# RWKV mixer stages: two products move from GpSimd to VectorE, the norm's matmuls stand between the solve's scores, and parts of the next block's work stand between the recurrence's steps

## The chip, the core and the metric

The kernel runs on one core of a Trainium2 chip. Its engines are PE (TensorE), DVE (VectorE), ACT (ScalarE), POOL (GpSimd) and SP (SyncE, which here only starts DMAs). The metric is the device time of one execution in microseconds; before the change it is 3907.61 us, the median of 3 runs (3906.08 to 3911.87).

## What is computed

The program is a stack of two different two-layer blocks over 512 tokens of width 1024, with feed-forward parts of width 2816 before, between and after the mixers. Nearly all of its time is projections. The part at hand is one mixer of the second layer, RWKV-7, with 8 heads of 64:

```python
def rwkv7_mixer(p, mu, w0, wB, a0, aB, gB, k_k, k_a, r_k, ln_g, ln_b):
    p = token_shift(p, mu)
    r, k, v, wd, ad, gd = split_cols(p, RK_SIZES)
    w_raw = -jax.nn.softplus(-(w0 + jnp.tanh(wd) @ wB)) - 0.5
    decay = jnp.exp(-jnp.exp(w_raw))
    a = jax.nn.sigmoid(a0 + ad @ aB)
    kk = heads(k * k_k); kk = kk / jnp.maximum(jnp.sqrt(jnp.sum(kk * kk, -1, keepdims=True)), 1e-12)
    k = k * (1.0 + (a - 1.0) * k_a)
    def step(state, inp):
        sa = jnp.einsum('bhij,bhj->bhi', state, -kk_t)
        state = (state * w_t[:, :, None, :] + sa[..., None] * (kk_t * a_t)[:, :, None, :]
                 + v_t[..., None] * k_t[:, :, None, :])
        return state, jnp.einsum('bhij,bhj->bhi', state, r_t)
```

Beside it stands a gated linear attention (GLA), whose output o gets a norm over each head: `head_norm(o, norm_g, None, eps) * silu(og)`.

## The kernel before

The recurrence over 512 tokens is done in chunks of C = 32 tokens, four chunks to a block of P = 128, NB = 4 blocks. Inside a chunk the dependence of each token on those before it is a triangular system, which is solved for all heads and chunks at once. Four stages do this, `rwkv_features`, `rwkv_solve`, `rwkv_chunks` and `rwkv_output`; a stage is a block of the program, and none starts before all engines are through with the one before. Within a stage each engine has its own list of instructions, in the order in which the code writes them, and waits on semaphores (`wait_ge`), which others raise (`then_inc`). All data of these stages lie in one tile, `odd_arena`; `bank` are the eight banks of PSUM.

**Features.** For k in 0 to 3 (128 rows of features each) ACT computes gates, an inverse norm RN and exponentials of the summed decays (CE, CP, CI; `decays`, L1930 and on). DVE sums and multiplies: `early(k)`, then `keys(k)` (KD and BI, L1990, L1992), `factors(k)` (key times CI, BI times CI, L1997, L1999) and `bonus(k)` (L1984, from PSUM). POOL multiplies r by CE (L2019) and KD by CP (L2021). CE has two slots, so ACT's decays of k wait until r of k - 2 is scaled. PE ends with 16 matmuls that compute nothing that is used (`warm`, L400).

**Solve.** PE computes four sets of scores (L2045), two banks each, and DVE multiplies the 32x32 triangles by a mask into LT (L2113, eight instructions a set). A set writes over the banks of the last but one, so the third and fourth wait for masks. Then PE does the norm of GLA's output: for each of four heads a matmul that centres it (L2052) and one of the mean square (L2057), with ACT squaring, copying and computing the factor (L2068 to L2083, two tables of functions in turn) and POOL applying it in three products (L2098, L2100, L2103). DVE meanwhile sets T to the identity (L2116, L2118), transposes LT (L2120), and solves: 31 times a product (L2126) and a subtraction (L2129), each waiting for the last, then a transpose (L2131). PE ends with 27 filling matmuls.

**Recurrence.** For a block b of 128 tokens PE's `before(b)` computes the scores of keys against KD (`scores(b, 0)`, L2166) and transposes KD, B2 and K2 (`turn`, L2178); ACT copies each transpose out (L2268) and DVE masks the scores to M (`mask_scores`, L2329). `front(b)` transposes the values (`turn(b, 3)`), computes the two other sets of scores (A1, A2 after DVE's mask), and three products that ACT copies out (L2290). `steps(b)` runs the four chunks in order: W1 times state (L2220), DVE's SA (L2352), keys times values (L2226) and BT times SA (L2231) into bank 4, DVE's sum to the next state (L2358). POOL scales the state by the decay (L2317). `output(b)` adds into banks 5 and 2 the product of values with A2 (L2242), of SA with A1 (L2245), and of states with r (L2251); ACT copies them out (L2273). The order on PE is before(0), and for each b front(b), steps(b), before(b + 1), output(b). DVE at a block's start spreads the solved triangles into the block-diagonal BD (four copies, L2337) and masks the scores.

## Time and profile before

| | |
|---|---|
| median of 3 runs | 3907.61 us (3906.08 to 3911.87) |
| the profiled execution | 3906.92 us, its span 3905.2 us |
| busy share of the span | PE 94%, DVE 44%, ACT 35%, POOL 16% |
| mean granted TensorE clock | 0.966 of full |

The engines work side by side, so shares don't add up. A share over the whole span tells little of a stage in which the engines wait for one another; for these the profile is cut into stretches and read as a timeline. The granted clock is that of TensorE alone: 1.00 is 2.4 GHz and 0.50 is 1.2 GHz. A busy PE isn't a PE at its peak: at half clock the same matmuls are busy twice as long. The profile splits an f32 matmul into two records, so that 8 matmuls are counted x16.

### The profile page before, as it was taken

The numbers are of one execution on the slowest core, as the hardware profiler recorded it, in microseconds if no ns is written. First come the engines' busy times: TensorE is split into PE (matmuls) and PEld (weight loads), VectorE is DVE, ScalarE is ACT, GpSimd is POOL, SyncE is SP. The second block draws the span as 40 slices with busy tenths as digits, with TensorE's granted clock in tenths as the row PEclk, the third lists the DMA queues.
The fourth block names the chain that finished last, engine by engine and source line by source line (L and its number), as shares of the span: only waits on it lengthen the run. The fifth ranks groups of instructions, "written<-read, shape, count | busy, mean of one in ns | idle before, by whom it ended". The sixth has DMA issues, their size and how long they took to land. (4 is left out here: it accounts for less than half of the span.)

```text
span 3905.2 us, 46147 instructions
## 1 busy us (share of the span) xinstructions
PE 3680.2 (94%) x18324; PEld 2992.0 (77%) x18324; DVE 1712.0 (44%) x2060; ACT 1369.7 (35%) x1828; POOL 624.7 (16%) x519
## 2 busy tenths in 40 slices
PE   8999987999999999887999989998999899989998
PEld 6888865888888887465888868786888787867886
DVE  2224564322422244753422344555663435547642
ACT  2223533422332243422422243345343423454432
POOL 2112002210311030130311140003111210022110
PEclk9999998999999999887999999999999999999999
DMA  3222211222222222000222233312222323222222
GB/s 140 97 84 88 92 54 65 76 97 88 95 97 97 89 98 87 18 1 23 76 97 87 91 123 104 113 65 97 97 97 87 118 98 119 79 100 81 97 92 81
DMA packets 62088, 340.09 MB, mean 87 GB/s; under 512 B 7024, under 2 KB 11520, under 8 KB 32768
## 3 DMA queue, kind: packets, MB, share of 16 engines
q1 hardware_dynamic: 61952, 338.19, 24.6%
q8 instruction: 96, 1.57, 0.2%
q14 instruction: 40, 0.33, 0.0%
HBM read 331.87 MB, written 6.29 MB: 87 GB/s over the span
## 5 line engine op out<-in xcount | busy, mean ns | idle before, releaser
L390 PE MATMUL bank<-x_hi,w_hi 128*128 128x512 f32 (+1 forms) x3360 | 1326.5, 395 | 107.3 <-POOL x_lo L2479 48.2
L391 PE MATMUL bank<-x_lo,w_hi 128*128 128x512 f32 (+1 forms) x3360 | 1313.0, 391 | 0.0
L392 PE MATMUL bank<-x_hi,w_lo 128*128 128x512 f32 (+1 forms) x3360 | 1312.2, 391 | 0.0
L354 DVE TENSOR_TENSOR w_lo<-raw,w_hi 128x2048 fp32r<-128x2048 f32 (+2 forms) x316 | 666.7, 2110 | 911.4 <-ACT w_hi L349 896.7
L390 PEld LDWEIGHTS bank<-x_hi,w_hi 128*128 128x128 f32 x3360 | 638.7, 190 | 266.5 <-issue 99.7
L349 ACT ACTIVATE w_hi<-raw 128x2048 fp32r<-128x2048 f32 (+2 forms) x311 | 538.9, 1733 | 715.2 <-PE bank L392 709.7
L392 PEld LDWEIGHTS bank<-x_hi,w_lo 128*128 128x128 f32 x3360 | 638.4, 190 | 132.6
L391 PEld LDWEIGHTS bank<-x_lo,w_hi 128*128 128x128 f32 x3360 | 639.1, 190 | 128.9 <-issue 1.0
L390 PE MATMUL bank<-f_g_hi,w_hi 128*128 128x512 f32 (+1 forms) x770 | 288.2, 374 | 0.0
L392 PE MATMUL bank<-f_g_hi,w_lo 128*128 128x512 f32 (+1 forms) x770 | 285.6, 371 | 0.0
L391 PE MATMUL bank<-f_g_lo,w_hi 128*128 128x512 f32 (+1 forms) x770 | 285.6, 371 | 0.0
L912 DVE TENSOR_TENSOR f_prod<-f_silu,bank 128x512 f32<-128x512 f32 x88 | 60.5, 688 | 453.9 <-ACT f_silu L865 453.9
L865 ACT ACTIVATE f_silu<-bank 128x512 f32<-128x512 f32 x88 | 52.8, 599 | 579.1 <-PE bank L392 579.1
L953 POOL TENSOR_TENSOR f_g_lo<-f_prod,f_g_hi 128x512 f32 (+1 forms) x88 | 114.0, 1295 | 805.0 <-ACT f_g_hi L867 805.0
L391 PEld LDWEIGHTS bank<-f_g_lo,w_hi 128*128 128x128 f32 x770 | 145.0, 188 | 26.2 <-issue 1.0
L390 PEld LDWEIGHTS bank<-f_g_hi,w_hi 128*128 128x128 f32 x770 | 145.1, 188 | 26.0 <-issue 1.0
L392 PEld LDWEIGHTS bank<-f_g_hi,w_lo 128*128 128x128 f32 x770 | 145.0, 188 | 24.8
L390 PE MATMUL bank<-c_g_hi,w_hi 128*128 128x512 f32 x352 | 137.2, 390 | 4.8 <-DVE w_lo L354 4.8
L391 PE MATMUL bank<-c_g_lo,w_hi 128*128 128x512 f32 x352 | 137.0, 389 | 0.0
L392 PE MATMUL bank<-c_g_hi,w_lo 128*128 128x512 f32 x352 | 136.9, 389 | 0.0
L3236 ACT ACTIVATE work<-bank,cols 128x512 f32<-128x512 f32 x88 | 63.7, 775 | 180.9 <-DVE bank L3281 180.9
L3334 POOL TENSOR_TENSOR c_g_lo<-work,c_g_hi 128x512 f32 (+1 forms) x44 | 56.9, 1295 | 424.6 <-ACT c_g_hi L3245 424.6
(443 smaller groups left out, 3988.3 us busy)
## 6 DMA issues: line engine op xcount, KB each, us to landing
raw<-in_weights SPq DMA_DIRECT2D x222, 1024.0 KB, 4.8
raw<-in_weights SPq DMA_DIRECT2D x96, 704.0 KB, 4.1
raw<-in_weights SPq DMA_DIRECT2D x8, 768.0 KB, 4.2
x_kept<-X SPq DMA_DIRECT2D x2, 2048.0 KB, 10.9
X<-x_kept SPq DMA_DIRECT2D x2, 2048.0 KB, 10.0
work<-in_rpb SPq DMA_DIRECT2D x12, 256.0 KB, 5.1
stats<-in_rpb SPq DMA_DIRECT2D x12, 256.0 KB, 5.3
X<-in_x SPq DMA_DIRECT2D x8, 256.0 KB, 6.2
```

What stands on the lines that cost most here:

```text
L349: act.activation(w_hi[:, s, 0:size], raw[:, s, 0:size], ACT.Copy).then_inc(hi_ready.sem, 1)
L354: dve.tensor_tensor(w_lo[:, s, 0:size], raw[:, s, 0:size], w_hi[:, s, 0:size].bitcast(F32), ALU.subtract).then_inc(lo_ready.sem, 1)
L390: pe.matmul(out, wh[:, w], hi(k), start=first and n == 0, stop=False, skip_group_check=not group)
L391: pe.matmul(out, wh[:, w], lo(k), start=False, stop=False, skip_group_check=not group)
L392: mm = pe.matmul(out, wl[:, w], hi(k), start=False, stop=last and n == len(kts) - 1, skip_group_check=not group)
L865: act.activation(silu[:, u, :], bank[2 * u][:, :], ACT.Silu).then_inc(act_ready.sem, 1)
L912: dve.tensor_tensor(prod[:, u, :], silu[:, u, :], bank[2 * u + 1][:, :], ALU.mult).then_inc(product_ready.sem, 1)
L953: pool.tensor_tensor(g_lo[:, j, :], prod[:, u, :], g_hi[:, j, :].bitcast(F32), ALU.subtract).then_inc(rest_ready.sem, 1)
L3236: act.activation(out[:, u, :], bank[2 * u + n][:, :], ACT.Identity, bias=ccol("conv_b_2", l * 2 * FT + off + j), scale=ccol("conv_w_2", (l ...
L3334: pool.tensor_tensor(g_lo[:, j, :], prod[:, u, :], g_hi[:, j, :].bitcast(F32), ALU.subtract).then_inc(rest_ready.sem, 1)
```

## The change

Four edits in three stages. (1) Features: POOL's two products per k are issued by DVE, inside `factors`; POOL has no work there. (2) Solve, PE: after each set of scores b comes the centring matmul of head b, and the mean square of head b - 1; the last mean square follows. (3) Solve, DVE: the two memsets of T stand before the masks. (4) Recurrence: the output's first eight matmuls (`values`) stand behind the first step, the next block's first scores behind the second and third in halves, the first transpose behind the fourth; DVE spreads one of the next block's four triangles after each step's state, and after the fourth masks the next scores. These scores use banks 1 and 7 in place of 0 and 1, so the second transpose, which writes bank 7, waits for the mask.

```diff
                     def factors(k):
-                        key, ci = RK[:, 4 + k, :], CI[:, k, :]
+                        r, key, ci = RK[:, k, :], RK[:, 4 + k, :], CI[:, k, :]
                         dve.wait_ge(decay_ready.sem, decay_ready.at(k + 1))
+                        dve.tensor_tensor(r, r, CE[:, k % 2, :], ALU.mult).then_inc(r_scaled.sem, 1)
                         dve.tensor_tensor(key, key, ci, ALU.mult)
                         dve.wait_ge(h_ready.sem, h_ready.at(k + 1))
+                        dve.tensor_tensor(KD[:, k, :], KD[:, k, :], CP[:, k, :], ALU.mult).then_inc(rest_ready.sem, 1)
                         dve.tensor_tensor(BI[:, k, :], BI[:, k, :], ci, ALU.mult)
-                @block.gpsimd
-                def _(pool):
-                    for k in range(4):
-                        r = RK[:, k, :]
-                        pool.wait_ge(product_ready.sem, product_ready.at(k + 1))
-                        pool.wait_ge(decay_ready.sem, decay_ready.at(k + 1))
-                        pool.tensor_tensor(r, r, CE[:, k % 2, :], ALU.mult).then_inc(r_scaled.sem, 1)
-                        pool.wait_ge(h_ready.sem, h_ready.at(k + 1))
-                        pool.tensor_tensor(KD[:, k, :], KD[:, k, :], CP[:, k, :], ALU.mult).then_inc(rest_ready.sem, 1)
...
+                    def centre(h):
+                        pe.wait_ge(centred.sem, centred.at(h - 1))
+                        pe.matmul(bank[4 + h % 2][:, :], const["centre_p"], OG[:, h, :], start=True, stop=True)\
+                            .then_inc(mean_ready.sem, 1)
+
+                    def mean_square(h):
+                        pe.wait_ge(square_ready.sem, square_ready.at(h + 1))
+                        pe.wait_ge(scale_ready.sem, scale_ready.at(2 * h - 2))
+                        pe.matmul(bank[6 + h % 2][:, :], const["mean_p"], sq[:, h % 2, :], start=True, stop=True)\
+                            .then_inc(square_used.sem, 1)
...
+                        centre(b)
+                        if b:
+                            mean_square(b - 1)
+                    mean_square(H4 - 1)
                     pe.wait_ge(masked.sem, masked.at(2 * NB))
                     warm(pe, 0, 27)
...
                     ch = Chain(dve, dve_chain)
+                    ch.add(dve.memset(T[:, :, :], 0.0))
+                    ch.wait()
+                    ch.add(dve.memset(T[:, :, :].rearrange("p s t -> p (s t)")[:, 0::C + 1], 1.0))
                     for g in range(2 * NB):
...
+            score_banks = ((1, 7), (2, 3), (4, 5))
...
-                    def before(b):
-                        pe.wait_ge(h_ready.sem, h_ready.at(4 * b))
-                        scores(b, 0)
-                        for x in range(3):
-                            turn(b, x)
+                    def values(b):
+                        for h in TURNS:
+                            pe.matmul(o(b, h, slice(0, P)), VT[:, cells(h)], A2[:, h, :], start=h % 4 == 0, stop=False,
+                                      skip_group_check=True)
+
+                    def beside(b, c):
+                        if c == 0:
+                            values(b)
+                        elif b + 1 < NB and c < 3:
+                            scores(b + 1, 0, TURNS[4 * c - 4:4 * c])
+                        elif b + 1 < NB:
+                            turn(b + 1, 0)
...
                             mm.then_inc(psum_ready.sem, 1)
+                            beside(b, c)
...
-                    before(0)
+                    scores(0, 0)
+                    turn(0, 0)
+                    pe.wait_ge(masked.sem, masked.at(1))
+                    turn(0, 1)
+                    turn(0, 2)
                     for b in range(NB):
                         front(b)
                         steps(b)
                         if b + 1 < NB:
-                            before(b + 1)
+                            pe.wait_ge(masked.sem, masked.at(3 * b + 4))
+                            turn(b + 1, 1)
+                            turn(b + 1, 2)
                         output(b)
...
+                    def spread(b, c):
+                        p = slice(C * c, C * c + C)
+                        return dve.tensor_copy(BD[p, :, p], TT[p, :, 8 * b:8 * b + 8].rearrange("p t h -> p h t"))
...
                             dve.tensor_tensor(ST[:, (g + 1) % 5, :], bank[4][:, 0:256], DS[:, :], ALU.add)\
                                 .then_inc(state_ready.sem, 1)
+                            if b + 1 < NB:
+                                ins = spread(b + 1, c)
+                                if c == 3:
+                                    ins.then_inc(frame_ready.sem, 1)
+                                    mask_scores(b + 1, 0)
```

## Rows read from the trace of the kernel before

**Rows 1.** Three stages: stretch, length, busy of PE, PEld, DVE, ACT, POOL, clock, DMA
```profile
1592.60:1636.40 43.80, 35.09 (x64) 12.26 (x64) 38.35 (x48) 23.80 (x41) 13.14 (x8) 0.77 0.02 4
1636.40:1687.70 51.30, 41.75 (x134) 20.46 (x134) 46.76 (x98) 24.73 (x32) 16.24 (x12) 0.80 0.00 1
1687.70:1814.70 127.00, 110.47 (x1600) 97.39 (x1600) 40.83 (x89) 21.45 (x36) 22.95 (x49) 0.76 0.01 2
```

**Rows 2.** Timeline of the features stage: start, us, engine, line, operation, tiles, count
```profile
1615.65 0.68 DVE L1990 TENSOR_TENSOR odd_arena<-odd_arena 128x512 f32<-128x512 f32 x1
...
1617.72 15.41 PE L400 MATMUL bank<-X,consts 128*128 128x512 f32 x32
...
1618.77 1.64 DVE L1992 TENSOR_TENSOR odd_arena<-odd_arena 128x512 f32<-128x512 f32 x1
...
1628.38 0.68 DVE L1984 TENSOR_TENSOR odd_arena<-bank,odd_arena 128x512 f32<-128x512 f32 x1
...
1634.26 0.68 DVE L1999 TENSOR_TENSOR odd_arena<-odd_arena 128x512 f32<-128x512 f32 x1
1634.86 1.27 DVE L1984 TENSOR_TENSOR odd_arena<-bank,odd_arena 128x512 f32<-128x512 f32 x2
```

**Rows 3.** Timeline of the solve stage; in brackets idle time before, and releaser
```profile
1636.43 2.56 PE L2045 MATMUL bank<-odd_arena 64*128 64x128 f32 x32 [3.31 <-PEq L437]
1637.60 9.73 DVE L2113 TENSOR_TENSOR odd_arena<-bank,odd_arena 32x128 f32<-32x128 f32 x32 [1.47 <-PE bank L2045]
...
1644.52 3.73 PE L2052 MATMUL bank<-odd_arena,mixer_consts 128*128 128x512 f32 x4
...
1647.61 0.91 DVE L2116 MEMSET odd_arena<- 128x1024 f32 x1 [0.28 <-issue]
...
1648.73 1.97 DVE L2120 STREAM_TRANSPOSE odd_arena<-odd_arena 128x1024 f32<-128x1024 f32 x1
...
1653.39 1.27 POOL L2098 TENSOR_TENSOR odd_arena<-odd_arena 128x512 f32<-128x512 f32 x1 [20.80 <-ACT odd_arena L2077]
1653.55 1.28 DVE L2126 TENSOR_TENSOR odd_arena<-odd_arena 128x156 f32<-128x156 f32 x1
...
1661.90 24.95 PE L400 MATMUL bank<-X,consts 128*128 128x512 f32 x54
```

**Rows 4.** Timeline of the recurrence: start of block 0, steps of block 1
```profile
1690.60 0.66 PE L2178 MATMUL bank<-consts,odd_arena 128*128 128x128 f32 x4 [1.08 <-POOL odd_arena L2306]
1690.82 1.29 DVE L2329 TENSOR_TENSOR odd_arena<-bank,odd_arena 128x512 f32<-128x512 f32 x2
...
1732.68 0.64 PE L2220 MATMUL bank<-odd_arena 64*32 64x64 f32 x16 [0.69 <-ACT odd_arena L2290]
...
1735.44 0.64 PE L2220 MATMUL bank<-odd_arena 64*32 64x64 f32 x16 [0.53 <-DVE odd_arena L2358]
...
1745.13 2.08 PE L2166 MATMUL bank<-odd_arena 64*128 64x128 f32 x16
1745.25 0.42 DVE L2358 TENSOR_TENSOR odd_arena<-bank,odd_arena 128x256 f32<-128x256 f32 x1 [1.22 <-PE bank L2231]
1745.59 1.51 DVE L2337 COPY odd_arena<-odd_arena 32x256 f32<-32x256 f32 x4
```

**Rows 5.** PE alone in three stretches: its busy time, then the granted clock, DMA
```profile
1638.00:1639.00 1.00, 0.99 (x10) 0.50 0.00 0
1736.90:1750.40 13.50, 12.41 (x144) 0.50 0.01 1
1750.50:1763.00 12.50, 11.20 (x180) 1.00 0.01 3
```

**Rows 6.** DVE's lines by form, solve: busy us, mean ns
```profile
L2126 DVE TENSOR_TENSOR odd_arena<-odd_arena 128x156 f32<-128x156 f32 x2 | 1.6, 804 | 0.1
```

**Rows 7.** Timeline of the recurrence: copies and values of the last block
```profile
1775.89 1.87 DVE L2337 COPY odd_arena<-odd_arena 32x256 f32<-32x256 f32 x4
...
1806.93 1.98 PE L2242 MATMUL bank<-odd_arena 128*64 128x128 f32 x16
```

More of the change, by code:

```diff
@@ L2115, in _ @@
                         ins.then_inc(masked.sem, 1)
-                    ch.add(dve.memset(T[:, :, :], 0.0))
-                    ch.wait()
-                    ch.add(dve.memset(T[:, :, :].rearrange("p s t -> p (s t)")[:, 0::C + 1], 1.0))
                     dve.wait_ge(masked.sem, masked.at(2 * NB))
@@ L2160, in _, with scores @@
                 def _(pe):
-                    def scores(b, x):
+                    def scores(b, x, turns=TURNS):
                         tok = slice(b * P, (b + 1) * P)
                         lhs, lk, rhs, rk = ((RK, 4, KD, 0), (BI, 0, RK, 0), (RK, 4, RK, 0))[x]
-                        for h in TURNS:
+                        for h in turns:
                             f, k = heads(h)
-                            mm = pe.matmul(bank[2 * x + h // 4][:, (h % 4) * P:(h % 4) * P + P],
+                            mm = pe.matmul(bank[score_banks[x][h // 4]][:, (h % 4) * P:(h % 4) * P + P],
                                            lhs[f, lk + k, tok], rhs[f, rk + k, tok], start=True, stop=True)
-                        mm.then_inc(score_ready.sem, 1)
+                        if turns[-1] == TURNS[-1]:
+                            mm.then_inc(score_ready.sem, 1)
                     def turn(b, x):
@@ L2179, in turn, with o @@
                         mm.then_inc(vt_psum.sem, 1)
-                    def before(b):
-                        pe.wait_ge(h_ready.sem, h_ready.at(4 * b))
-                        scores(b, 0)
-                        for x in range(3):
-                            turn(b, x)
+                    def o(b, h, cols):
+                        f, k = heads(h)
+                        return bank[5 - 3 * (h // 4)][f, k * P + cols.start:k * P + cols.stop]
+                    def values(b):
[9 more added lines that the diff above has]
+                            turn(b + 1, 0)
                     def front(b):
@@ L2233, in steps @@
                             mm.then_inc(psum_ready.sem, 1)
+                            beside(b, c)
                     def output(b):
-                        def o(h, cols):
-                            f, k = heads(h)
-                            return bank[5 - 3 * (h // 4)][f, k * P + cols.start:k * P + cols.stop]
                         for h in TURNS:
-                            pe.matmul(o(h, slice(0, P)), VT[:, cells(h)], A2[:, h, :], start=h % 4 == 0, stop=False,
-                                      skip_group_check=True)
-                        for h in TURNS:
-                            pe.matmul(o(h, slice(0, P)), SA[:, cells(h)], A1[:, h, :], start=False, stop=False,
+                            pe.matmul(o(b, h, slice(0, P)), SA[:, cells(h)], A1[:, h, :], start=False, stop=False,
                                       skip_group_check=True)
```

24 lines of the change are left out of this document (6 added, 18 removed).

## The prediction

> **What bounds the kernel now.** The page is read first: PE is busy 94% of the span, but that is an average over projections that stream weights, and the change lies elsewhere, in three stages of the odd layer's RWKV mixer. So the second view is the table of stretches [rows 1]. The features stage takes 43.8 us, the solve 51.3 us and the recurrence 127.0 us, 222.1 us or 5.7% of the span, at a mean clock of 0.77 to 0.80. No weights arrive in them, and what they lose or gain is passed on whole, since the next stage starts only when all engines are through. The third view is the timeline of each stage, read from its end backwards. In the features stage DVE works without a gap up to its last instruction, which starts at 1634.86 for 1.27 us and so ends at 1636.13; PE starts the next stage 0.30 us later [rows 2, 3]. PE's own last work, the filling matmuls, ended at 1617.72 + 15.41 = 1633.13 [rows 2]. In the solve DVE again sets the time: 32 masks, two memsets, a transpose and a loop of 62 small instructions, each waiting for the one before it. In the recurrence the set-up and output between steps are a chain on PE, and the steps go back and forth between PE and DVE.
>
> **Features.** The change takes eight products (L2019, L2021) from POOL and puts them on DVE. What they cost DVE now is seen beside them: with both inputs in SBUF, DVE's L1992 takes 1.64 us beside POOL, while L1984, which reads a PSUM bank, takes 0.68 us beside POOL, and L1999 alone takes 0.68 us with the next start 0.60 us later [rows 2]. After the change POOL does nothing here. From 1615.65, where L1990 starts this part [rows 2], DVE has 16 + 8 + 4 = 28 instructions at 0.60 us, 16.8 us, plus 0.12 us for each of four dependent pairs and 0.17 us for waiting for ACT's second exponential, plus 0.08 us since the last one's duration exceeds the pitch: 17.5 us, end 1633.2 instead of 1636.13. The new waits cost nothing: ACT's third and fourth decays wait for the r products of the first and second group, which are done by 1619.2 and 1622.9, and the fourth decay (needed at 1629.5) ends some 5 us early. Gain **2.9 us**. PE's filling matmuls end at 1633.13, so nothing more could be had. Bounds: 2.5 to 3.0 us.
>
> **Solve, set-up of T.** The two memsets stand now between masks and transpose, 1647.61 to 1648.73, 1.12 us [rows 3]. They move to the stage's start, where DVE waits until 1637.60 for the first scores and the memset (0.9 us) fits. Gain 1.1 us.
>
> **Solve, norm between the scores.** PE's order becomes scores 0, centre, scores 1, centre, mean square, scores 2, centre, mean square, scores 3. A set of scores takes 2.08 us at half clock, 1.04 at full (the next scores have the same shape and were timed at half clock [rows 4]); the norm's four first matmuls took 3.73 us across half clock, so one is 0.86 to 0.93 us at full. The idle time of PE ahead of the stage shrinks from 3.3 us to 0.3 us. Before, PE's clock had fallen by 1638.0 [rows 5], 1.6 us into the stage; with the gap gone I take full clock. Scores 3 are then done 4 x 1.04 + 5 x 0.88 + 0.2 = 8.8 us into the stage; DVE, which starts 1.17 us in and needs 9.73 / 4 = 2.43 us a set, wants them at 8.5 us. Loss 0.35 us.
>
> The norm starts some 7 us earlier against the masks. Its first POOL product came 8.9 us after its first matmul (1644.52 to 1653.39), so now at about 9.2 us into the stage; the masks last until 11.3 and the transpose, which reads one tile, until 13.3. Two of the twelve POOL products, 1.3 us each, end by 11.9. Twelve loop instructions of DVE are now stretched by such products: the form 128x156 took 1.28 us [rows 3] against a mean of 0.804 over its two [rows 6], so 0.33 alone, a loss of 0.95 us each. The masks read PSUM and by L1984 aren't stretched. Gain 2 x 0.95 = 1.9 us. Solve in sum: **-1.1 + 0.35 - 1.9 = -2.6 us**; bounds -3.5 (one more product hidden) and -0.7 (none).
>
> **Recurrence, first block.** The second and third transposes now wait for the mask of the first scores, 1690.82 + 1.29 = 1692.11; the second ran at 1690.60 [rows 4]. The third ran only at 1692.2 anyway, so one group of four transposes, 0.55 us at full clock, is added. The stage may also start at half clock: the filling matmuls of the solve (24.95 us from 1661.90 [rows 3]) start with the norm's end, now some 7 to 8 us earlier, while the loop ends only some 3 us earlier, so PE idles about 5 us before the recurrence instead of 0.9. Much of this hides behind the mask's wait. The row of before has no such start; bounds 0 and 1.7 us, I take 0.7. Sum **+1.25 us**.
>
> **Recurrence, steps.** A step at full clock lasts 1732.68 to 1735.44, 2.76 us, of which PE waits 0.53 us for the state at its end [rows 4]. What is put there costs its own time less that cover. The values (1.98 us at half clock [rows 7], 0.99 at full) stand after the first step, mostly at full: +0.45. Half a set of scores is 1.04 us at half clock: +0.5, twice. The first transpose stands after the fourth step, where PE has no wait now: 0. DVE's copies of the triangular blocks, 1.51 us for four [rows 4], so 0.38 each, come after the state's sum; the next use of DVE is over 0.7 us later, so they are hidden. Steps: +1.45 us a block.
>
> **Recurrence, between blocks.** Gone from PE: the scores, 2.08 us, and the values, 1.1 us as the clock rises there. Added: a wait. PE's second transpose waits for the mask of the next scores, which stands on DVE behind the last state sum and the last copy. After PE's last step matmul, at 1745.13, it is 0.12 us to the sum and 0.34 more to the copy [rows 4], 0.38 for it, 1.29 for the mask, 0.1 to PE, 2.23 us; the first transpose fills 0.97 of them; PE idles 1.26 us, and the other two transposes and the whole output are queued behind. The clock: in the second block the steps end on PE at 1745.13 [rows 4]; it was 0.50 from 1736.9 to 1750.4 and 1.00 from 1750.5 [rows 5], so it rose 5.3 us after the steps' end, and PE had worked without a gap till then. With a gap in it I expect the rise later, and a us of matmuls at half clock instead of full costs half a us; the bounds are no delay and two thirds of those 5.3 us again, 0 and 1.7 us of cost; I take 1.0. Sum -2.08 - 1.1 + 1.26 + 1.0 = -0.9 us. With the steps: **+0.55 us for each of three blocks, +1.65 us**. The fourth has no successor: values +0.45 in the step, -1.98 at the end at half clock: **-1.5 us**.
>
> **Sum.** -2.9 - 2.6 + 1.25 + 1.65 - 1.5 = -4.1 us. The profiled execution took 3906.92 us (span 3905.2 and 1.7 around it), 0.7 below the median of 3907.61. 3906.92 - 4.1 = 3902.8, and by the median 3903.5; I say **3903.0 us**.
>
> **Rivals.**
> - *Half clock is broken in the steps.* If the added matmuls hold the clock at full, each block's 13.5 us at half clock [rows 5] shrink by half of the matmul work in it less the waits between steps, which stay, some 4 us: 3903 - 4 x 4 = 3887. For it: the values stand right where the clock falls. Against it: PE shows 12.41 us busy in those 13.5 us [rows 5] and the clock stays at half, so busy time of such small matmuls doesn't raise it. The Trainium skill ("TensorE: Matmul & The Clock Gate", section "HAM oscillation — how this bites in real kernels") says that idle gaps between bursts of matmuls return the array to half clock, and that work closed up keeps it at full. By that rule this rival would win; the rows don't bear it out. Chance 0.07.
> - *The steps hide all.* The pieces fit in the waits and the clock rises no later: 3 x (0.95 + 1.0) = 5.9 us less, 3897. Chance 0.15.
> - *The solve turns from DVE to PE.* At half clock four scores and five norm matmuls take 4 x 2.08 + 5 x 1.75 = 17.1 us, and the last masks end at 19.5 instead of 10.9 us: +8.3, **3911**, slower than before. It decides if the clock falls before scores 2, about 4 us in. Against it is the closed gap. Chance 0.07.
> - *The clock rises too late.* If the new idle 1.26 us holds the rise until after the output, output, two transposes and next scores run at half: about +5 us a block, 3903 + 3 x 4.5 = 3916. Chance 0.05.
> - *DVE and POOL collide anew.* Each copy now starts beside POOL's product of the same state (L2317); after the third block's steps four copies took 1.87 us with one such product started among them, against 1.51 [rows 4, 7]. The copy starts first, so POOL should wait, which nobody notices. If DVE loses 0.36 us in each of 12 places, part of it under cover, and the solve's two products aren't hidden: +4, 3907. The Trainium skill ("SBUF — State Buffer", section "Who interferes with whom") says that whichever starts first takes the shared port for its whole instruction: by it the copy wins and the cost is nil. Chance 0.06.
> - The forecast as worked out keeps 0.60. Its own range is 3899 to 3908: with every term at its good end (features -3.0, solve -3.5, first block +0.55, blocks -0.45 each, last -1.5) the sum is -8.8, at its bad end (-2.5, -0.7, +2.25, +1.25 each, -1.5) +1.3.
>
> **How the numbers follow.** A measurement can tell about 0.2%, 7.8 us, from no change: below 3899.8 or above 3915.4. Faster: the first rival 0.07, two thirds of the second 0.10, the forecast's edge 0.03, 0.20. Slower: half of the late rise, 0.03. Same: 0.77. The range 3894 to 3911 leaves out the first rival, the late rise, and the edges of the second and third, under 0.2.
>
> **What would show it.** Features: 24 two-input DVE products all at about 0.68 us, the stage 2.9 us shorter. Solve: memsets before the first mask, ten stretched loop instructions instead of twelve, PEclk 1.00 in the first 8 us. Recurrence: PE idle about 1.3 us after the first transpose behind the fourth step; first step 3.2 us; steps after the clock's fall 4.1 us instead of 3.6; the stage within 1.5 us of 127 + 1.4. Wrong would be: half clock in the solve's scores, or a clock at 1.00 through the steps.

## The result and the profile after

The changed kernel takes 3913.36 us (median of 22 runs, 3911.58 to 3917.28), the kernel before 3907.38 us in the runs beside it. The ratio is 1.0018, 95% interval 1.0012 to 1.0024: slower by 6 us (medians) to 7 us (ratio), where 3903.0 us, a gain of 4 us and a range of 3894 to 3911 us were forecast.

The two early stages came out as forecast, the recurrence did not. The stretches that answer to [rows 1], same columns:

```profile
1592.60:1633.50 40.90, 35.40 (x64) 12.43 (x64) 35.46 (x56) 23.88 (x41) 0.00 (x0) 0.75 0.02 4
1633.50:1682.60 49.10, 38.25 (x134) 17.82 (x134) 44.92 (x98) 24.73 (x32) 15.44 (x12) 0.90 0.00 1
1682.60:1813.50 130.90, 116.26 (x1600) 101.64 (x1600) 40.56 (x89) 21.35 (x36) 24.49 (x49) 0.72 0.01 2
```

The features stage is 2.9 us shorter, the solve 2.2, the recurrence 3.9 longer at a lower clock. PE does the same matmuls (800, counted x1600), but they take 116.26 us instead of 110.47 [rows 1]. Its idle time fell from 16.5 to 14.6 us, as the change means to; the lower clock took back three times as much.

The timeline of features and solve, against [rows 2, 3]:

```profile
1622.25 0.69 DVE L1997 TENSOR_TENSOR odd_arena<-odd_arena 128x512 f32<-128x512 f32 x1
...
1632.00 1.28 DVE L1984 TENSOR_TENSOR odd_arena<-bank,odd_arena 128x512 f32<-128x512 f32 x2
1633.59 1.16 PE L2049 MATMUL bank<-odd_arena 64*128 64x128 f32 x16 [0.41 <-PEq L437]
1633.83 0.91 DVE L2106 MEMSET odd_arena<- 128x1024 f32 x1 [0.55 <-PEq L437]
...
1642.94 2.40 DVE L2114 TENSOR_TENSOR odd_arena<-bank,odd_arena 32x128 f32<-32x128 f32 x8 [0.60 <-PE bank L2049]
...
1645.38 1.91 DVE L2118 STREAM_TRANSPOSE odd_arena<-odd_arena 128x1024 f32<-128x1024 f32 x1
...
1648.03 1.32 DVE L2127 TENSOR_TENSOR odd_arena<-odd_arena 128x60 f32<-128x60 f32 x1
```

Every product on DVE from 1615.4 us on takes 0.68 or 0.69 us, the memset lies ahead of the first mask, and ten loop instructions are stretched, to 1.20 to 1.35 us, the first of them the one at 1648.03.

**One trace was not enough.** The execution traced took 3917.18 us, 3.8 above the median. It stands 0.2 us behind the kernel before at 1917 us, and 10.3 us at the end, the rest lost in unchanged code. A second and a third trace (e12, e13 below) lose nothing there. They lose it in the recurrence, first the second trace, then the third:

```profile
1683.35:1822.74 139.39, 126.45 (x1601) 110.74 (x1601) 40.66 (x89) 21.34 (x36) 24.38 (x49) 0.65 0.01 2
```
```profile
1684.20:1823.55 139.35, 126.41 (x1601) 110.72 (x1601) 40.66 (x89) 21.36 (x36) 24.45 (x49) 0.65 0.01 2
```

That is taken as the usual execution: of four traces of this recurrence on the new solve (the fourth is e10 below, with the same recurrence), 130.9 us came once and 139.3 to 139.4 three times. The runs without a trace show only their mean clock; 17 of the 22 have 0.962 or 0.963, as the traces with 139 us do (0.962), and five 0.964 or 0.965, as the trace with 130.9 us does (0.964). The second trace has -4.4 us at the stage's start and +12.4 in it, 3914.65 us in all against the profiled 3906.92. Its first block, PE alone (start, us, idle time ahead in brackets):

```profile
1697.30 0.64 PE L2231 MATMUL bank<-odd_arena 64*32 64x64 f32 x16 [0.69 <-ACT odd_arena L2301]
1697.86 0.68 PE L2237 MATMUL bank<-odd_arena 32*64 32x64 f32 x16
1698.86 0.68 PE L2242 MATMUL bank<-odd_arena 32*64 32x64 f32 x16 [0.32 <-DVE odd_arena L2365]
1699.47 1.41 PE L2187 MATMUL bank<-odd_arena 128*64 128x128 f32 x16
1700.81 1.07 PE L2231 MATMUL bank<-odd_arena 64*32 64x64 f32 x16
...
1704.93 1.06 PE L2231 MATMUL bank<-odd_arena 64*32 64x64 f32 x16
...
1709.06 1.06 PE L2231 MATMUL bank<-odd_arena 64*32 64x64 f32 x16
...
1712.05 1.11 PE L2178 MATMUL bank<-consts,odd_arena 128*128 128x128 f32 x4
1714.38 1.97 PE L2178 MATMUL bank<-consts,odd_arena 128*128 128x128 f32 x8 [1.21 <-DVE odd_arena L2340]
1716.27 1.98 PE L2250 MATMUL bank<-odd_arena 128*64 128x128 f32 x16
1718.18 3.63 PE L2256 MATMUL bank<-odd_arena 64*64 64x32 f32 x64
...
1723.10 3.79 PE L2165 MATMUL bank<-odd_arena 64*128 64x128 f32 x32 [0.25 <-ACT odd_arena L2284]
```

PE waits 0.69 us for ACT's copy of the third product of the set-up (L2219), does one step at full clock, and the clock falls inside the values (1.41 us, between the 1.09 and 1.98 us of the two levels). Steps start 4.12 us apart, and transposes, output and the next scores all run at half (3.79 us for L2165; 2.06 at full). The same place as two stretches of PE (busy, clock):

```profile
1700.20:1727.30 27.10, 25.64 (x299) 0.50 0.01 2
1727.50:1734.10 6.60, 5.78 (x79) 1.00 0.01 2
```

The kernel before had 13.5 us of that per block [rows 5]. The fall itself comes only about 1 us earlier. In the first three blocks of three traces of the kernel before it came 1.1 to 4.4 us after the start of the first step, and the clock stayed at half for 13.6 to 17.1 us; in those of e12 and e13 it came 1.4 to 2.8 us after that start and stayed for 20.5 to 27.3 us. What grew most is the stay.

### The profile page after: what moved, and what is told of

It reads as the page before. It is cut to its first block and busy times, and to the rows that moved or that the text cites. A ratio compares the mean times of both kernels' runs of the same rounds, so it can differ in the third digit from the quotient of the medians.

```text
span 3915.5 us, 46143 instructions
## 1 busy us (share of the span) xinstructions
PE 3693.5 (94%) x18324; PEld 3000.6 (77%) x18324; DVE 1707.2 (44%) x2068; ACT 1370.1 (35%) x1828; POOL 612.8 (16%) x511
```

## The experiments

Offsets come from the starts of the same matmul in two traces. "Start" is the recurrence's first matmul (1687.77 before), "stage" the time from it to the next stage's first matmul, "half" the time at half clock from 1685 to 1820 us, "tail" what the offset changes by between 2402 us and the end. All in us, kernel before first. The fixed window of "half" takes in up to 26 us of the next stage where the stage is short; inside the stage alone it is 61.4 us before (64.5 in e14 and e15), 72.8, 98.4 and 98.4 in the three traces of the changed kernel, 40.5 in e5 and 36.0 in e4. Medians are compared with the kernel before as run beside them, which has four medians, 3906.1 to 3907.4; two more single runs of it, without a trace, took 3913.96 us (beside e13 to e15) and 3913.22 (beside e16 to e18).

```
kernel                       start   stage   half   tail   median (runs)
before             1st       0       127.0   64.9   0      3907.4 (22), 3906.1 (29), 3906.8 (24), 3906.3 (18)
e14 before         2nd      +2.1     126.2   68.3   0
e15 before         3rd      +0.4     126.2   68.3   0.1
changed            1st      -5.1     130.9   76.1  10.0    3913.4 (22)
e12 changed        2nd      -4.4     139.4   94.0   0
e13 changed        3rd      -3.6     139.3   94.0  -0.1
e1  features+solve          -5.1     125.7   65.4   6.2    3904.2 (12)
e2  recurrence only         +0.6     132.1   76.0   3.7    3914.8 (12)
e3  output first            -4.8     131.8   82.0  -0.2    3914.3 (12)
e16 output first   2nd      -6.5     138.9   94.0   0
e5  values ahead            -4.0     119.0   42.8   6.2    3899.0 (6)
e17 values ahead   2nd      -6.6     119.2   46.9  -0.1
e7  dummies                 -7.1     123.4   51.2   3.6    3904.5 (11)
e18 dummies        2nd      -4.1     126.8   63.0   6.8
e6  before, values ahead    -0.6     121.1   61.4   0.2    3904.1 (11)
e4  filled                  -4.9     111.1   46.3   0      3885.4 (6)
e9  filled rec. only        -2.0     116.4   51.2   0      3894.7 (7)
e8  before, delay 8         -1.4     126.8   68.3   3.6    3915.7 (7)
e11 before, delay 3         +3.1     126.8   66.7   6.8    3915.5 (11)
e10 changed, delay 3        -6.9     139.3   94.0   3.2    3921.0 (6)
```

**The change in two halves.** e1 keeps the recurrence of before, e2 has its new order alone.

> Only the features and the solve are changed (all feature products on VectorE, the norm between the solve's scores, the memsets ahead); the recurrence is that of the kernel before. Locally both theories expect the recurrence to begin 5.1 us earlier (in the changed kernel it began at 1682.71 instead of 1687.77). Theory 1 (the loss is in the recurrence's new order, the rest of the program only shifts): the recurrence takes 128.4 us as before and the total is 3907.4 - 5.1 = 3902.3 us, ratio 0.9987. Theory 2 (the unchanged stages behind change their time by several us according to where they meet the clock's falls): the start of the recurrence is 5.1 us earlier, yet the total is off 3902.3 by more than 2.5 us, and the time in which the granted clock stood at half behind 1850 us differs from the 58.0 us before by 5 us or more.

> Only the recurrence is changed (next scores, transposes and values between the serial steps); features and solve are those of the kernel before. In the changed kernel the stage took about 132 us from its first front to the next stage against 127 before (+4 us), because the clock was at half through the steps of three blocks and through what followed them, after a wait of 1.2 to 1.7 us for the mask of the first turn. Theory 1: the stage is 3 to 5 us longer here too and the total is 3907.4 + 4 = 3911.4 us, ratio 1.0010. Theory 2: the stage is 3 to 5 us longer, but the total is off 3911.4 by more than 2.5 us through the unchanged stages. A rival to the cause within the stage (that the clock's phase at its start decides, not the wait): in this kernel the stage starts 5 us later than in the changed one, and another set of blocks has the half clock; the stage would then be within 1.5 us of before.

e1: 3904.18 us, ratio 0.9991 (0.9982 to 0.9999), start -5.1 as expected, stage 125.7. e2: 3914.79 us, ratio 1.0020 (1.0010 to 1.0031), stage 132.1. The first half gains, the second costs more than it. In e2's trace the stage does not return to before's, so the rival, that only the moment of the stage's start decides, falls there; its total is 3.4 us above the expected 3911.4. Both have a tail: the trace of e1 lost 6.2 us behind 2402 us in code that is the same. The 58.0 us of half clock that the expectation gives for the kernel before reach only to about 3270 us; from 1850 us to the end it is 91.7 us, and 91.3 in e1. So e1 lost 6.2 us with no more half clock in all, only in other places.

**Which wait?** PE is idle in two spots around the steps: 1.2 to 1.7 us for the next block's first mask behind them (new), and 0.69 us for ACT's copy of the set-up's third product ahead of them (as before; the expectations call it the first product, but the copy waited for is that of L2219). e3 removes the first:

```diff
                         steps(b)
+                        output(b)
                         if b + 1 < NB:
                             pe.wait_ge(masked.sem, masked.at(3 * b + 4))
                             turn(b + 1, 1)
                             turn(b + 1, 2)
-                        output(b)
```

> The changed kernel with one difference: a block's output products stand behind its steps, ahead of the transposes that wait for VectorE's mask of the next block's first turn. In the changed kernel TensorE stood idle 1.2 to 1.7 us there (1707.5 to 1709.8 in the first block) and the clock fell at 1709.86. Theory 1 (that wait starts the low clock and costs its own length too): the wait is gone, 3 x 1.3 = 4 us at the least, and half clock in the recurrence falls from 72.9 us to 61 or less; total 3913.4 - 4 = 3909 us or below. Rival (the clock falls anyway in the steps, behind the wait for ScalarE's copy): only part of the idle time comes back, since output products run at half clock instead: 3911 to 3913 us, half clock in the recurrence 70 us or more.

Median 3914.28 us, ratio to before 1.0019 (1.0010 to 1.0028), no better than the changed kernel and above both expectations. Its traced execution took 3906.4 us, 8 below that median, hence a second trace:

> The kernel of e3 profiled again. Its first trace had a recurrence of 131.8 us and took 3906.4 us, 8 us below its median of 3914.3. If TensorE's wait for the mask of the next first turn is not what lets the clock fall, the usual execution has the changed kernel's 139 us, and 3912 to 3915 us in all. If that wait was the cause, the recurrence is again near 132 us.

```profile
1681.29:1820.23 138.94, 127.17 (x1601) 111.64 (x1601) 40.72 (x89) 21.10 (x36) 24.38 (x49) 0.65 0.01 2
```

Usual execution: 139 us again. PE idles 1.2 us less than in the changed kernel (138.94 - 127.17 = 11.8 against 139.39 - 126.45 = 12.9) and its matmuls take 0.7 us more. In its first block the clock came back 15.2 us behind the steps, as in e12, with no wait for the mask there (only PE's wait for ACT's copy of the output is longer, 0.81 us against 0.25). So the wait for the mask isn't the cause.

e5 fills the other spot with work that is there anyhow: the third product (L2219 in the changed kernel) goes to bank 6, which leaves banks 2 and 5 free for the values. ACT reads it from there (that line isn't shown; `...` in the `matmul` stands for its unchanged last arguments).

```diff
-                            mm = pe.matmul(bank[2][:, cells(h)], BD[:, h, :], U[:, cells(h)], ...)
+                            mm = pe.matmul(bank[6][:, cells(h)], BD[:, h, :], U[:, cells(h)], ...)
                         mm.then_inc(attended.sem, 1)
-                        pe.wait_ge(u_ready.sem, u_ready.at(3 * b + 3))
                         pe.wait_ge(masked.sem, masked.at(3 * b + 3))
+                        values(b)
+                        pe.wait_ge(u_ready.sem, u_ready.at(3 * b + 3))
...
                         if c == 0:
-                            values(b)
+                            pass
```

> The changed kernel with one difference in the recurrence: a block's eight value products stand ahead of TensorE's wait for ScalarE's copy of the first product (0.69 us idle), not behind the first serial step; TensorE still waits 1.2 to 1.7 us for the mask of the next block's first scores, and the next scores still stand between the steps. Theory (the idle time at the copy, just ahead of small products, is what lets the clock fall in the steps): three blocks of 26 to 28 us where the changed kernel had 35.4 and 32.8, half clock in the recurrence below 60 us instead of 76, total 3895 to 3903 us. Rival (the wait for the mask, or the length of the steps, does it): blocks of 31 to 35 us in two of three, total 3909 to 3913 us.

> The kernel of e5 profiled again. If the idle time at the wait for ScalarE's copy is the cause, the recurrence stays between 117 and 124 us (119.0 in its first trace) in every execution. If its first trace was a lucky one, it is 131 or 139 us as in the changed kernel.

Median 3899.02 us, ratio 0.9969 (0.9957 to 0.9981). Both traces:

```profile
1683.74:1802.77 119.03, 103.35 (x1601) 89.90 (x1601) 40.47 (x89) 21.34 (x36) 24.39 (x49) 0.83 0.01 2
```
```profile
1681.17:1800.41 119.24, 104.03 (x1600) 90.35 (x1601) 40.43 (x89) 21.36 (x36) 24.39 (x49) 0.81 0.01 2
```

Moving eight matmuls per block by one step takes 20 us from the stage. The time of the same matmuls falls by 22 to 23 us, while PE idles more than in the changed kernel (15.7 against 12.9 us). The block's steps of the first of the two traces:

```profile
1724.53 1.09 PE L2187 MATMUL bank<-odd_arena 128*64 128x128 f32 x16
1725.56 0.64 PE L2232 MATMUL bank<-odd_arena 64*32 64x64 f32 x16
...
1728.32 0.64 PE L2232 MATMUL bank<-odd_arena 64*32 64x64 f32 x16 [0.53 <-DVE odd_arena L2372]
...
1731.06 1.03 PE L2232 MATMUL bank<-odd_arena 64*32 64x64 f32 x16
```

The values stand directly ahead of the steps; the clock falls in the third step instead of behind the first. It does so in two blocks of this trace, and in the other two only 9.6 and 12.7 us after the first step's start.

e7 leaves the order alone and puts useless work in the same spot, which tells the clock from the order:

```diff
                         mm.then_inc(attended.sem, 1)
+                        for h in TURNS[:4]:
+                            pe.matmul(bank[6][:, cells(h)], BD[:, h, :], U[:, cells(h)], start=True, stop=True)
                         pe.wait_ge(u_ready.sem, u_ready.at(3 * b + 3))
```

> The changed kernel with four extra products (128 by 128 with 64 columns each, their result overwritten and used by none) ahead of TensorE's wait for ScalarE's copy of the first product: work of 1.0 us at full clock in a wait of 0.69 us, order and everything else unchanged. Theory (the clock falls because TensorE is idle there): the added work costs 0.3 us a block, 1.2 us in all, yet the clock stays up in the steps of two or three blocks, each worth 3 x 1.4 us: total 3900 to 3908 us, below the changed kernel. Rival (the clock has nothing to do with that wait): the total is that of the changed kernel plus 1.2 us, 3914 to 3915 us, and the steps behind the fall take 4.1 us as there.

> The kernel of e7 profiled again (extra products in the wait for the copy, order unchanged). If the idle time there is the cause, the recurrence stays between 120 and 127 us (123.4 in its first trace). If not, 131 or 139 us plus 1.2.

Median 3904.54 us, 9 us below the changed kernel, with 16 matmuls more (counted x32); against the kernel before the ratio is 0.9998 (0.9989 to 1.0007), so it only takes the loss back. The second block of its first trace:

```profile
1721.58 1.06 PE L2222 MATMUL bank<-odd_arena 128*128 128x64 f32 x8
1722.57 0.64 PE L2233 MATMUL bank<-odd_arena 64*32 64x64 f32 x16
...
1724.73 1.97 PE L2187 MATMUL bank<-odd_arena 128*64 128x128 f32 x16
1726.63 1.07 PE L2233 MATMUL bank<-odd_arena 64*32 64x64 f32 x16
...
1729.81 0.64 PE L2233 MATMUL bank<-odd_arena 64*32 64x64 f32 x16
...
1733.32 1.06 PE L2233 MATMUL bank<-odd_arena 64*32 64x64 f32 x16
```

The first row is the added work. The clock falls behind the first step all the same (values 1.97 us), but comes back 3.4 us later, for the third step; it falls again at 1731.6 us and is back at 1741.8. So do the third and the fourth block fall and come back, though the last fall then lasts 17.1 us; the first block has all four steps at full clock, as it also had in the changed kernel's first trace. The stage took 123.4 and 126.8 us, so work that nobody needs gained 13 to 16 us against the usual 139.4. This is the run that decides where the cause lies: little differs but that PE works ahead of the steps instead of waiting. It doesn't bear out the expected route, that the clock falls because of this idle time: the fall stayed in four blocks of the eight traced, and what shrank is the time at half clock.

e6 makes e5's move in the kernel before, with nothing between the steps:

> The kernel before with that one move alone: the values ahead of the wait for the copy, nothing between the serial steps, all next scores and transposes behind them. Theory (the idle time at the copy lets the clock fall, and what stands between the steps is worth its idle time): the wait of 0.96 us goes, at most 4 x 0.96 = 3.8 us; the steps still wait 0.84 us for VectorE at each turn, so part of the low clock stays: total 3896 to 3904 us. Rival (the gain of the filled kernel comes from work between the steps, since a step that waits 0.8 us in each turn loses the clock anyhow): half clock in the recurrence stays at 60 us or more and no more than the 3.8 us comes back: 3902 to 3906 us.

The stage is 5.9 us shorter in the trace (121.1), more than the 3.8 us at most, with 61.4 us at half clock: mostly the rival. Median 3904.11 us, ratio 0.9993 (0.9984 to 1.0002), so no change that can be told. Filling the wait alone is worth 5 to 6 us of the stage where the steps keep their waits for the next state (0.53 us); with work there it is worth 20 us. Read the other way: on the filled wait, the work between the steps takes only 2 us more from the stage (e5 119.0 against e6 121.1), one trace of e6, with the features and the solve of before, against two of e5; on the unfilled wait that work costs 12 us.

**A version that beats both.** e4 is e5 plus the output first (e3), with the next scores' halves beside steps 0 and 1 and the first transpose beside step 2. ACT's list is changed to match: it copies the first transpose ahead of the output, the others behind it (not shown).

```diff
-                        if c == 0:
-                            values(b)
-                        elif b + 1 < NB and c < 3:
-                            scores(b + 1, 0, TURNS[4 * c - 4:4 * c])
-                        elif b + 1 < NB:
+                        if b + 1 < NB and c < 2:
+                            scores(b + 1, 0, TURNS[4 * c:4 * c + 4])
+                        elif b + 1 < NB and c == 2:
                             turn(b + 1, 0)
```

> As the kernel with the output first, and the values of the block stand ahead of the wait for ScalarE's copy of the first product (in the changed kernel 0.69 to 0.79 us idle, just behind which the clock fell in three of four blocks), with the later serial steps carrying the two halves of the next scores and the first transposes. Theory 1 (the idle time ahead of the copy lets the clock fall, filling it holds it at full): steps at full clock, 2.75 us each as in the first block, not 4.13 us: 3 blocks x (3 x 1.4 + 1.3 + 0.7) = 18 us at most, half clock in the recurrence under 40 us; total 3895 to 3903 us. Rival (the serial steps themselves, small products with short waits, let it fall whatever stands ahead): steps of 4.1 us in two or three blocks, 1 to 5 us gained, 3908 to 3912 us.

Median 3885.44 us, ratio 0.9946 (0.9932 to 0.9959): 10 us below the expected range. One block's steps, and the stretch of PE around it:

```profile
1751.22 0.64 PE L2230 MATMUL bank<-odd_arena 64*32 64x64 f32 x16
...
1754.02 0.64 PE L2230 MATMUL bank<-odd_arena 64*32 64x64 f32 x16
...
1756.77 0.64 PE L2230 MATMUL bank<-odd_arena 64*32 64x64 f32 x16
...
1759.47 0.64 PE L2230 MATMUL bank<-odd_arena 64*32 64x64 f32 x16
```
```profile
1719.40:1780.70 61.30, 55.78 (x1000) 1.00 0.01 2
```

Two blocks on end without a fall, steps 2.70 to 2.80 us apart with the next scores inside; the first and the last block lose the clock, 6.8 and 5.7 us after their first step's start. Which of e4's differences from e5 brings the further 8 us of the stage was not tested apart. Whether it needs the solve's new order too:

> The filled recurrence of e4 (values ahead of the wait for the copy, halves of the next scores and the first transposes between the steps, output ahead of the wait for the mask) on the features and the solve of the kernel before. In e4 the offset against the kernel before was -4.9 us at the start of the recurrence and -20.8 us behind it. Additive: the recurrence's share is -15.9 us, total 3906.5 - 15.9 = 3890.6 us. Rival (e4's blocks stay at full clock only since the solve's new order starts the stage at another point against the clock's falls): one block or more keeps steps of 3.6 to 4.1 us, and the share is 6 to 12 us, total 3894 to 3901 us.

The median is 3894.72 us (3881.61 to 3901.83), ratio 0.9965 (0.9950 to 0.9980), the stage 116.4, a share of -10.6 us instead of -15.9. Total and share are the rival's, its sign isn't: steps start at most 3.14 us apart, and the clock falls late, in the fourth step of three blocks for 10.2 us each and in the third step of the last for 17.1. Whether the two halves of the change add up stays open, since the interval of seven scattered runs reaches from 3886.8 to 3898.5 us and has the additive 3890.6 us in it.

**The unchanged stages.** e8, e10 and e11 put products into the start of the output stage (`warm(pe, 0, 8)` or `3` ahead of the means).

> The kernel before with eight extra products of 512 columns (their result overwritten) at the start of the output stage behind the recurrence, a plain delay of about 3.4 us at full clock with nothing else changed. Theory 1 (what stands behind 1850 us only shifts): total = before + 3 to 4 us, and the offset against the kernel before is the same at 1917 us and at the end. Theory 2 (the stages from 2400 us on take some 4 to 10 us more or less according to where the clock's falls meet them; the changed kernel lost 10 us there and 0.2 us up to 1917 us): the offset at the end differs from that at 1917 us by more than 2.5 us in the trace, or the median by as much from before + 3.5 us.

> The kernel before with the same three extra products. Theory 1 (a plain shift): 3906.5 + 1.3 to 2.6 us = 3908 to 3909 us, and the offset at the end is that of 1917 us. Theory 2 (what stands behind 2400 us is worth 3.6 to 10 us more or less by its place in time, as with eight products, where the offset went from 5.2 to 8.7 us): another 2.5 us or more on top, 3911 us or above, or the same in the trace.

> The changed kernel with three extra products of 512 columns at the start of the output stage (their result overwritten), a delay: eight of them cost 6.9 us in the kernel before at half clock, so 1.3 to 2.6 us here. Theory (the 10 us that the changed kernel lost from 2400 us on hang on where the clock's falls meet unchanged stages): the loss there is another one than 10.0 us in the trace, by 2.5 us or more, and the total is off 3913.4 + 2 us by as much. Rival (the loss there comes with the changed kernel's own data or buffers, not with its place in time): 10 us again in the trace and 3915 to 3916 us.

The delays cost 6.9, 2.6 and 2.7 us where they stand, and the medians rose by 8.9, 9.2 and 7.6 us (against the kernel before in the same runs, and for e10 against the changed kernel's 3913.4). The tails were 3.6, 6.8 and 3.2 us. So what is lost behind 2400 us isn't fixed. One kernel differs from itself: e5 had a tail of 6.2 and of -0.1 in two executions, the changed kernel 10.0, 0 and -0.1. But the place in time moves the odds a great deal: ten of the eleven runs of e11 took 3913.8 us or more, where a plain shift would be 3908.9. PE around the first such place, first trace of the changed kernel, then its second:

```profile
2447.20:2451.20 4.00, 3.21 (x13) 0.50 0.02 4
```
```profile
2455.10:2459.10 4.00, 3.84 (x19) 1.00 0.02 4
```

Same code behind nearly the same idle time (2.81 and 2.61 us for DVE), once at half clock, once not. Second and third traces of both kernels ask what stands for the median:

> The changed kernel itself, profiled a second time. Its first trace stood at +0.2 us against the kernel before at 1917 us and at +10.3 us at the end (3917.2 us); 18 of its 22 times lie between 3911.6 and 3914.6 us. If the loss up to 1917 us belongs to the code, the second trace has it within 1 us of +0.2. If the loss behind 2400 us belongs to the single execution in part, it comes out as another one: +6 us for a time near 3913.4 us.

> The changed kernel, profiled a third time. Theory A (the recurrence with its new order usually has the half clock in the steps of all four blocks, +12 us, and the loss behind 2400 us is an accident of the first trace): offset about +8 us at 1917 us and at the end, 3912 to 3915 us, 94 us of half clock between 1685 and 1820 us. Theory B (the stages behind 2400 us carry the median's loss): +0.2 us at 1917 us and +6 us or more at the end.

> The kernel before, profiled again. Theory A: its recurrence takes what it took (127.0 us from its first front product to the next stage's first product, 65 us of half clock between 1685 and 1820 us), within 1.5 us, and nothing is lost behind 2400 us for a time near 3907 us. Theory B: behind 2400 us it gains or loses several us against its first trace, as often as the changed kernel does.

> As the run ahead of it: theory A has the recurrence at 127 us within 1.5 us for a third time; theory B has the offset behind 2400 us at 3.6, 6 or 10 us.

e12 missed its first expectation: the offset at 1917 us was +7.8 us instead of +0.2, so the +0.2 belonged to the single execution and not to the code. Its loss behind 2400 us was another one, as expected, namely none. e13 to e15 bear out theory A: e13 has +8.6 us at 1917 us and +8.4 at the end, with 94.0 us at half clock (3915.36 us in all, just above the range), e14 and e15 have the stage within 1.5 us of 127 and no tail, though with 68.3 us at half clock instead of 65. Stage 139.4 and 139.3 us in the changed kernel (139.3 in e10 too), 126.2 to 127.0 in five traces of the kernel before with and without delay (125.7 in e1), and no tail in e12 to e15.

## Why the prediction was wrong

**Right.** Features: -2.85 us against -2.9, each product at 0.68. Solve: -2.2 against -2.6; ten stretched instructions; the masks waited 0.31 and 0.60 us for the last two sets of scores, 0.91 in sum where 0.35 us of loss was forecast, which is about what the gain fell short by; and PE at full clock for 14.7 us:

```profile
1633.60:1648.30 14.70, 11.22 (x78) 1.00 0.00 0
```

The 3911 us rival (turning from DVE to PE) did not come. The first step at full clock with the values behind it took 3.20 us (first trace, block 0), as forecast. PE's new idle time was 1.21 us against 1.26 in e12's first block (1.66 in that of the first trace). Copies on DVE weren't stretched (0.36 to 0.37 us each in block 0 of the first trace) and hid: DVE was idle for 0.38 to 0.89 us before its next work in the steps. POOL's product, started just behind two of these copies, took 0.81 and 0.82 us against 0.62 before, and nothing waited for it.

**First block.** +1.25 us forecast; from the stage's first matmul to the first step it takes 13.95 us in all three traces of the changed kernel, against 14.65 in the first trace of the kernel before (-0.70), but 13.05 and 13.08 in e14 and e15 (+0.9). The start at half clock came as it was put in. In the three traces the clock was back at full 3 us into the stage; in e10 only after 9.8 us, and there the block took 16.06 us. So against two of the three traces this term is near the forecast's size. The -0.70 comes from the first one, where the clock was at half from 1692.4 to 1695.9, later in the set-up than in those two (about 0.2 to 3.7 us into the stage).

**Steps: the term that failed.** +1.45 us a block, from full clock in the first step and the fall where it was. In e12, the usual execution, the four steps take 14.75, 15.75 and 14.77 us instead of 12.47, 12.45 and 12.33: +2.3, +3.3, +2.4. The distances of 4.1 us were forecast; that the clock falls within 1.5 to 2.8 us of the first step's start in every block, so that the inserted values are paid at half clock in part or in whole, was not.

**Between blocks: the term that failed most.** -0.9 us forecast; +2.9, -0.8, +2.5 measured (20.67, 17.15, 20.64 against 17.79, 17.97, 18.18 us). The forecast took 1.0 us for a later rise, 1.7 at most, reckoned from the 5.3 us in which the clock had come back after the steps. It came back 15 us after them in the first and the third block (1712.05 to 1727.4 in the first), behind transposes, output and the next scores, and 6 us after them in the second, which is the one with -0.8. The last block, -1.5 forecast, cost +0.6 for the same reason: all output at half (L2256 3.63 us). Sum of the stage: -0.7 + 8.0 + 4.6 + 0.6 = +12.5, measured +12.4, forecast +1.4. These differences are against the first trace of the kernel before; against e14 and e15, whose stage is 0.8 us shorter, it is +13.2.

**The right rival had 0.05.** "The clock rises too late", 3916 us, describes this: blocks +5.2, +2.5 and +4.9 us, where it had +4.5 each. Its trigger was wrong: it named the wait for the mask, and without that wait the stage takes 138.9 us (e16). The spot is the 0.69 us ahead of the steps, which stood in [rows 4] all along and which the forecast left out, as an old wait that the change leaves alone. Filled, the stage takes 119.0 and 119.2 us (e5) or 123.4 and 126.8 (e7) instead of 139.4. The steps keep their clock longer in e5; in e7 it falls as before in four blocks of eight and comes back sooner.

**The rival of 3887 us had 0.07**, and was dismissed with 12.41 us busy of 13.5 at half clock [rows 5]. The row is right, and so are 25.64 of 27.10 us above: such work doesn't bring the clock back. But it says nothing on whether the same kinds of matmuls keep a clock that hasn't fallen, and e4 shows that they can, 55.78 us busy in 61.30 at full. Its time, 3885.4 us, is near what that rival worked out, but for another kernel, so the nearness is luck. The Trainium skill ("TensorE: Matmul & The Clock Gate", section "HAM oscillation — how this bites in real kernels") says that gaps between bursts of matmuls return the array to half clock and that work closed up keeps it at full. In the example there the Trainium skill has waits of some 3 to 5 us for a DMA. None of the idle spots around the steps is as long (0.69 us ahead of the steps, 0.2 to 0.5 in them, 1.2 to 1.7 behind them), and the clock falls. That closing gaps helps, e5 and e4 agree with; e7 agrees in part only, since there the clock falls behind the closed gap. The half-clock stretches of 27 us have next to no gaps in them (25.64 us busy of 27.10), so gaps alone don't account for their length.

**Open.** Why the clock, once it has fallen in the steps, stays at half for 13.6 to 17.1 us in the first three blocks of the kernel before and for 20.5 to 27.3 us in the changed one, behind the same 0.69 us; and by which route filling that spot shortens the stay in e7. That the spot matters is shown by filling it; that idle time there makes the clock fall is not. Work inserted into waits should have helped; without the filled spot it didn't. Nor is it known what makes one execution of the changed kernel 130.9 us and three 139.3, or what sets the tails of 3 to 10 us.

## What to carry to other kernels

Before work is put between the serial steps of a loop, look at where the clock falls in the loop, and at PE's last idle spot ahead of it: what is inserted behind the fall is paid at double, and so is the work behind it for as long as the clock stays low. Try to fill that spot first, with products whose inputs are ready, if need be by moving one result to another bank; here that was worth 13 to 20 us of a stage of 139, by a route that stays open. A forecast of a few us needs the clock's course at full and at half for the whole stretch, and an explanation needs two or three traces: the first trace here put the loss in the wrong stage.

## What the hardware showed that was not expected

- Useless matmuls made the changed kernel faster: 1.06 us of them a block, 3904.5 against 3913.4 us (medians of 11 and of 22 runs). They did not make it faster than the kernel before.
- A clock that has fallen can come back after 3.4 us (e7) or after 27.3 us (e12), behind the same first step and with the same matmuls in the steps.
- Half clock held for 27.1 us with PE busy for 25.64 of them (e12), and full clock for 61.3 us with 55.78 (e4).
- One kernel has several executions: the stage took 130.9 us once and 139.3 to 139.4 in three others, and unchanged code from 2402 us to the end took 0, 3 to 4, 6 to 7 or 10 us more in different traces.
